# A hybrid decoder step: the compressed branch's rows stored column by column, its position bias made a column of the same matmuls

## The reference, cut to what matters

```python
def compress(rows, pos_emb, w1, w2):
    idx = np.arange(n_cmp)[:, None] * CMP_STRIDE + np.arange(CMP_LEN)[None, :]
    blocks = rows[:, idx] + pos_emb[:, None, :]
    flat = blocks.transpose(0, 1, 3, 2, 4).reshape(B, n_cmp, KV, CMP_LEN * HD)
    return jax.nn.gelu(flat @ w1) @ w2
```

## Time and profile before

| | |
|---|---|
| time, median of 3 executions | 2914.3 us (2913.38, 2914.3, 2918.69) |
| profiled execution, first to last instruction | 2918.1 us; the time of this same execution apart from the three above isn't given, and its span lies at their upper end |
| PE busy | 2805.5 us, 96% of the span, 17763 matmuls |
| PE weight loads busy | 2651.7 us, 91% |
| DVE, POOL, ACT busy | 1577.8 us (54%), 788.6 us (27%), 472.0 us (16%) |
| mean granted TensorE clock | 0.941 of full speed |
| DMA | 380.73 MB, mean 130 GB/s |

### The profile page before, as it was taken

How to read it: one execution, slowest core, us unless ns; L and a number is a source line. 1 busy time by engine, 2 the same in 40 slices (tenths; PEclk the granted TensorE clock), 3 DMA queues, 4 the chain that set the end, 5 groups by cost and what they waited for, 6 DMA issues and landing times. The chain is left out here.

```text
span 2918.1 us, 45487 instructions
## 1 busy us (share of the span) xinstructions
PE 2805.5 (96%) x17763; PEld 2651.7 (91%) x17763; DVE 1577.8 (54%) x1539; ACT 472.0 (16%) x1106; POOL 788.6 (27%) x579
## 2 busy tenths in 40 slices
PE   7999999999999999999898998979999999999997
PEld 6999999799999969998586777969999999999996
DVE  4555555355555564453655544555565565555555
ACT  2110000111000130000523542031100000000002
POOL 1321332133233620000433101633323322322353
PEclk9999999999999999999656777979999999999998
DMA  6555555355555445663331113535455555545542
GB/s 178 154 153 157 155 138 148 103 151 153 156 153 139 121 106 145 153 147 87 130 97 33 48 47 94 137 85 146 136 165 145 145 143 158 150 133 163 152 131 84
DMA packets 734087, 380.73 MB, mean 130 GB/s; under 512 B 65402, under 2 KB 729722, under 8 KB 733386
## 3 DMA queue, kind: packets, MB, share of 16 engines
q1 hardware_dynamic: 733754, 378.60, 47.2%
q10 hardware_dynamic: 272, 1.36, 0.1%
HBM read 370.60 MB, written 13.38 MB: 132 GB/s over the span
## 5 line engine op out<-in xcount | busy, mean ns | idle before, releaser
L292 PE MATMUL bank<-xh_before,wh_before 128*128 128x320 f32 x2112 | 657.2, 311 | 11.3 <-DVE wl_before L310 11.3
L293 PE MATMUL bank<-xl_before,wh_before 128*128 128x320 f32 x2112 | 655.0, 310 | 0.0
L294 PE MATMUL bank<-xh_before,wl_before 128*128 128x320 f32 x2112 | 655.0, 310 | 0.0
L292 PE MATMUL bank<-xh_after,wh_after 128*128 128x320 f32 x1664 | 521.5, 313 | 22.1 <-DVE wl_after L310 13.6
L308 DVE CAST wh_before<-raw 128x2048 fp32r<-128x2048 f32 (+1 forms) x196 | 219.2, 1119 | 596.6 <-PE bank L294 565.4
L293 PE MATMUL bank<-xl_after,wh_after 128*128 128x320 f32 x1664 | 518.5, 312 | 0.0
L294 PE MATMUL bank<-xh_after,wl_after 128*128 128x320 f32 x1664 | 518.4, 312 | 0.0
L310 DVE TENSOR_TENSOR wl_before<-raw,wh_before 128x2048 fp32r<-128x2048 f32 (+1 forms) x196 | 464.0, 2368 | 6.7
L308 DVE CAST wh_after<-raw 128x2048 fp32r<-128x2048 f32 (+1 forms) x168 | 184.9, 1101 | 436.0 <-PE bank L294 435.5
L310 DVE TENSOR_TENSOR wl_after<-raw,wh_after 128x2048 fp32r<-128x2048 f32 (+1 forms) x168 | 409.4, 2437 | 5.8
L292 PEld LDWEIGHTS bank<-xh_before,wh_before 128*128 128x128 f32 x2112 | 398.7, 189 | 13.3 <-issue 8.6
(11 more groups left out here) (232 smaller groups left out, 3436.0 us busy)
## 6 DMA issues: line engine op xcount, KB each, us to landing
raw<-in_w_ffn_in SPq DMA_DIRECT2D x176, 1024.0 KB, 5.8
raw<-in_w_ffn_out SPq DMA_DIRECT2D x128, 704.0 KB, 4.8
raw<-in_w_in SPq DMA_DIRECT2D x36, 1024.0 KB, 5.7
raw<-in_w_in SPq DMA_DIRECT2D x16, 512.0 KB, 5.2
raw<-in_w_out SPq DMA_DIRECT2D x16, 512.0 KB, 4.3
raw<-in_w_out SPq DMA_DIRECT2D x64, 128.0 KB, 3.9
proj<-in_cache_cmp_kv SPq DMA_DIRECT2D x64, 64.0 KB, 2.5
raw<-in_state_gla SPq DMA_DIRECT2D x8, 512.0 KB, 4.5
```

The costliest lines, as they stand in the source:

```text
L292: pe.matmul(out, L.wh[a][:, w], hi[:, k], start=(k == 0), stop=False)
L293: pe.matmul(out, L.wh[a][:, w], lo[:, k], start=False, stop=False)
L294: last = pe.matmul(out, L.wl[a][:, w], hi[:, k], start=False, stop=(k == nk - 1))
```

## The change

`R` is stored in another order. Before, a pair of rows m = 8 j + r of a head lay at column m, so that the 15 columns of a matmul's step were 8 apart. After, the tile is `R[r, block, j]`: 8 planes r, in each 33 groups of 16 columns j. Step l reads plane l % 8, from column l // 8 on, 15 neighbouring columns from each group. ACT's take writes the new order, so that neighbouring elements of its input go to 8 planes, 33 * 16 columns apart.

The 33rd group is for the position bias. POOL clears it once (after the first stage of ffn1), and ACT puts the 16 columns of the turned position embedding into columns 0 and 1 of it (`place_pos`), for the keys at place h = 0 and for the values at place h = 4. The 16 matmuls then have 33 * 15 = 495 columns, of which column 480 is the bias, the next ones not used. The 16 one-column matmuls and their bank are gone. ACT's copy of the bias now waits for the 495-column matmuls.

```diff
-        self.R = flat[:, 5120:9216].rearrange("p (b k m) -> p b k m", b=NB, k=KV)
+        self.R = flat[:, 4992:9216].rearrange("p (r b j) -> p r b j", r=8, j=16)
...
         pe.wait_ge(self.w_in, 16 * (n + 1))
-        pe.wait_ge(self.pos_taken, 1)
+        pe.wait_ge(self.pos_placed, n + 1)
         if n:
             pe.wait_ge(self.acted, 1)
-            pe.wait_ge(self.bias_taken, 1)
-        for l in range(LT):
-            mm = pe.matmul(L.bank[7][:, 0:1], self.w1[:, l], self.posT[:, n * LT + l:n * LT + l + 1],
-                           start=(l == 0), stop=(l == LT - 1))
-        mm.then_inc(self.biased, 1)
         pe.wait_ge(self.taken, NB * (n + 1))
         for l in range(LT):
-            mm = pe.matmul(L.bank[6][:, 0:NB * KV * NC], self.w1[:, l],
-                           self.R[:, :, :, l:l + 8 * (NC - 1) + 1:8].rearrange("p b k n -> p (b k) n"),
-                           start=(l == 0), stop=(l == LT - 1))
+            mm = pe.matmul(L.bank[6][:, 0:(NB * KV + 1) * NC], self.w1[:, l],
+                           self.R[:, l % 8, :, l // 8:l // 8 + NC], start=(l == 0), stop=(l == LT - 1))
         mm.then_inc(self.hidden, 1)
+
+    def gpsimd(self, pool):
+        pool.memset(self.R[:, :, NB * KV], 0.0).then_inc(self.cleared, 1)
+
+    def place_pos(self, act, n):
+        row = self.R[:, :, NB * KV, 0:2].rearrange("p r j -> p j r")
+        act.activation(row, self.posT[:, n * 16:(n + 1) * 16].rearrange("p (j r) -> p j r", r=8), ACT.Copy
+                       ).then_inc(self.pos_placed, 1)
...
             act.activation(self.posT, L.bank[6][:, 0:32], ACT.Copy).then_inc(self.pos_taken, 1)
+            act.wait_ge(self.cleared, 1)
+            act.wait_ge(self.pos_taken, 1)
+            self.place_pos(act, 0)
         for j in (2 * h, 2 * h + 1):
             act.wait_ge(self.turned, j + 1)
             if j == NB:
                 act.wait_ge(self.hidden, 1)
-            act.activation(self.R[:, j % NB].rearrange("p k m -> p (k m)"), L.bank[2 + j % 4][:], ACT.Copy
+                self.place_pos(act, 1)
+            b = j % NB
+            act.activation(self.R[:, :, b * KV:(b + 1) * KV].rearrange("p r k j -> p k j r"),
+                           L.bank[2 + j % 4][:].rearrange("p (k j r) -> p k j r", k=KV, r=8), ACT.Copy
                            ).then_inc(self.taken, 1)
...
-        act.wait_ge(self.biased, n + 1)
-        act.activation(L.cmp_bias[:, n:n + 1], L.bank[7][:, 0:1], ACT.Copy).then_inc(self.bias_taken, 1)
+        act.wait_ge(self.hidden, n + 1)
+        act.activation(L.cmp_bias[:, n:n + 1], L.bank[6][:, at:at + 1], ACT.Copy).then_inc(self.bias_taken, 1)
         act.wait_ge(self.bias_taken, n + 1)
-        act.wait_ge(self.hidden, n + 1)
```

More of the change, by code:

```diff
@@ L336, in __init__ @@
             L.sem("blocks_" + x) for x in ("turned", "taken", "hidden", "acted", "pos_turned", "pos_taken"))
-        self.biased, self.bias_taken = L.sem("blocks_biased"), L.sem("blocks_bias_taken")
+        self.pos_placed, self.bias_taken, self.cleared = (
+            L.sem("blocks_" + x) for x in ("pos_placed", "bias_taken", "cleared"))
     def load_w1(self, sp, n):
@@ L421, in scalar_hidden @@
     def scalar_hidden(self, act, n):
-        L = self.L
-        act.wait_ge(self.biased, n + 1)
-        act.activation(L.cmp_bias[:, n:n + 1], L.bank[7][:, 0:1], ACT.Copy).then_inc(self.bias_taken, 1)
+        L, at = self.L, NB * KV * NC
+        act.wait_ge(self.hidden, n + 1)
+        act.activation(L.cmp_bias[:, n:n + 1], L.bank[6][:, at:at + 1], ACT.Copy).then_inc(self.bias_taken, 1)
         act.wait_ge(self.bias_taken, n + 1)
-        act.wait_ge(self.hidden, n + 1)
-        act.activation(L.hid[n][:, 0:NB].rearrange("p b k n -> p (b k n)"), L.bank[6][:, 0:NB * KV * NC],
+        act.activation(L.hid[n][:, 0:NB].rearrange("p b k n -> p (b k n)"), L.bank[6][:, 0:at],
                        ACT.Gelu_apprx_tanh, bias=L.cmp_bias[:, n:n + 1]).then_inc(self.acted, 1)
@@ L534, in _ @@
                                            ALU.subtract).then_inc(L.hidden_made, 1)
+                    if side and c == 0:
+                        side.gpsimd(pool)
                     if c < CH - 1:
```

## The result

The changed kernel takes 2897.86 us (median of 7 runs, 2881.06 to 2903.11), the kernel before, on the same chip, 2916.39 (7 runs, 2905.34 to 2920.68). The ratio is 0.9934 [0.9914, 0.9954]: 19.2 us faster, 13 to 25 by the interval. The forecast was 2891.5, a gain of 22.8; the time lies 0.86 us above the upper end of the range.

A forecast was written before the change was run, and what follows sets the result against it. PE, busy for 96% of the span, was taken to bound ffn1 and projection. Gains of 16.0 us at h = 3 and 6.8 us in projection, 22.8 in all, from 2914.3 gave 2891.5 us, range 2885 to 2897.

The forecast's parts named there:

- Wide matmuls: PE's matmuls in the new order, at h = 3 and in projection: 0.413 us a record, 13.2 us for 32.
- the layout does not help: Rival: the gap after each 15 words is as dear as a hop; only 3.4 us gained, 2910.9 us; chance 0.05.
- Takes: ACT's 512-element takes, now storing scattered words: 0.47 us more each, off the path at seven of eight places.
- h = 3: Place in ffn1 where PE waits directly for both takes: piece ends at 527.85 instead of 543.82, 16.0 us gained.
- The slower rival: Scattered stores in ACT's takes use up the gain at 6.4 us a take; at 7, 6.6 us slower; chance 0.03.
- Projection: Second unit waits for the layer norm's low parts and its split: 9.65 us gained, less 2.8 for the clock, net 6.8.
- the clock holds: Rival: PE's clock does not fall in projection's second unit; 25.6 us gained, 2888.7 us; chance 0.15.
- the rival that all adds up: PE's microseconds at h = 3 and in projection simply add up: 33.8 us gained, 2880.5 us; chance 0.04.
- Sum: Total of h = 3 (16.0 us) and projection (6.8 us): 22.8 us gained, 0.78%.
- From there on DVE is a unit ahead as before: After projection's second unit, DVE's next split ends 3.6 us after 1060.13; PE needs it 7.04 us or more after.
- later stages whose own lengths change by more than 2 us, which nothing above accounts for: Sign named in advance that the prediction is wrong, for stages behind the changed places: own lengths changing by over 2 us.
- 0.9 under and 4.4 over: Spread in us of the earlier kernel's runs about their median, used with the terms' ends for the range 2885 to 2897.

The follow-up runs named there:

- the layout alone: The changed kernel with the 16 one-column bias matmuls kept and 480-column wide ones, rows in the new order: 2895.63 us, ratio 0.9917 to the kernel before.

## Where the prediction held, and where it failed

The sum came out where it was made, up to projection's third split. What failed is the step from there to the time of the program: that all behind it moves rigidly, at no cost, and the scatter that the range gave to it.

- **Wide matmuls**: 0.413 us forecast, 0.416 found. The gaps after each 15 words cost nothing that can be seen, the rival "the layout does not help" fell.
- **Takes**: 0.47 us more forecast, 0.48 found, at no cost but at h = 3. The slower rival needed 6.4 us a take.
- **h = 3**: 16.0 forecast, 16.1 found. What I had not seen: some 2 us of this need the one-column matmuls gone, and with them the clock's drop at this place; the layout alone gained 12.4 here. The sum priced the new records at full clock without asking for it, and was right there by luck.
- **Projection**: 9.65 us less 2.8 for the clock, 6.8 forecast. Found: 10.0 less 1.9 for the clock, and 1.0 less for the norm's sums, which the sum had not; over seven profiles 6.6 to 7.2 in all. The rival "the clock holds" fell with the window from 1034.90 (0.74); the rival that all adds up fell with the two kernels that take away and double the values' matmuls.
- **Sum**: 22.8 forecast, 22.5 and 23.3 found in the two profiles of the change, to the third split.
- **Failed**: not "From there on DVE is a unit ahead as before" itself, which projection's further splits bear out (281.60 us in each profile), but the silent step behind it, that all that lies after moves rigidly by 22.8 us, and the range that counts the scatter from three runs of before, "0.9 under and 4.4 over". The prediction named the test itself, "later stages whose own lengths change by more than 2 us, which nothing above accounts for": one did, by 5.2. PE runs there at a mean clock of 0.80 to 0.83, and how much of it falls to the lower level differs between executions of one program by tens of us, with 0.37 us of length for each of them. Runs lie up to 12 us from their mean before and up to 16 after; of the change's 16, 3 are at 2880 to 2881, 12 at 2896 to 2903, and one near the forecast's 2891.5. The range was narrow even by its own figures: 2895.0 for the dearer ends of the terms and 4.4 for the runs make 2899.4, and 2897 was given.

The median lies 6.4 us over the forecast. Of these 2.1 lie in the kernel before, whose median was 2914.3 with 3 runs and is 2916.39 with 7, and 4.3 in the gain. With all 16 runs of the change the mean gain is 18.7 us. That is 21.4 at equal clock less 2.7 for more time at the lower level behind the third split: of the 15.6 +- 13.4 us more, 6.8 lie ahead of that split, where the traces show them and the sum had its 2.8 us for the clock, and 8.8 behind it. These 8.8 are not clear of zero, so that no run shows the change to lengthen the later stretch; that it doesn't is not shown either. Whether the place in time at which this work ends shifts the odds of the clock's falls further on stays open.

## What to carry to other kernels

A part taken out of the bounding engine's queue is worth what lies between it and the next thing that is late: here 16.1 of some 17.6 us at one place and 7 of some 17.6 at the other, both readable ahead of time from the rows of what would be late next. Where a stage has a mean granted clock between the two levels, executions of one program can differ by more than the change is worth (here 22 us over 60 runs, against a gain of 18.7). Count the scatter from many runs, and compare at equal clock before explaining a difference in a stage that was not touched. Leave out of that correction the low time that the change itself moves: it is part of the effect.

## What the runs showed that I had not expected

Matmuls of one column, dense in PE's queue for 4.0 us, were followed by a clock of 0.50 although the trace shows PE busy for 2.00 of 2.00 us in the window. A moving operand fetched eight words apart costs 0.86 to 0.88 us for 480 columns at 0.50 and 0.858 at 1.00, while one with neighbouring columns goes from 0.406 to about 0.85. A copy of 128x512 from a bank to single words takes 1.03 us on DVE and 1.07 on ACT.
